# A gated convolution layer on one core: the second root spread goes from four exact products to two rounded ones, and the low halves of the output weights change engines

## The reference, cut to what matters

```
hn = x * rsqrt(mean(x*x) + eps) * norm_g
a, b, gate = split(hn @ w_in)                # 1024 x 3072
u = conv(a * sigmoid(b))                     # depthwise, 31 taps, causal
u = silu(layernorm(u)) * silu(gate)
y = x + u @ w_out                            # 1024 x 1024
```

## Time and profile before

| | |
|---|---|
| median of 3 runs | 363.22 us (363.17 to 363.48) |
| the profiled execution | 363.72 us, its span 361.9 us |
| TensorE busy | 356.9 us, 99% of the span |
| VectorE busy | 319.9 us, 88% |
| GpSimd busy | 269.8 us, 75% |
| ScalarE busy | 232.4 us, 64% |
| granted TensorE clock | 1.00 of full speed |

### The profile page before, as it was taken

How to read it: one execution, slowest core, us unless ns; L and a number is a source line. 1 busy time by engine, 2 the same in 40 slices (tenths; PEclk the granted TensorE clock), 3 DMA queues, 4 the chain that set the end, 5 groups by cost and what they waited for, 6 DMA issues and landing times.

```text
span 361.9 us, 4758 instructions
## 1 busy us (share of the span) xinstructions
PE 356.9 (99%) x1564; PEld 289.2 (80%) x1564; DVE 319.9 (88%) x514; ACT 232.4 (64%) x334; POOL 269.8 (75%) x194
## 2 busy tenths in 40 slices
PE   7999999999999999999999999999999999999996
PEld 6888888888888888888888888888888888888885
DVE  4779799999999899999999998993798979997952
ACT  5889685558847772998667875975655951452400
POOL 0029999999999997899999999795796532359220
PEclk9999999999999999999999999999999999999999
DMA  7995011201411311406112214235713695066042
GB/s 260 403 400 206 34 60 58 91 28 58 116 60 53 65 60 58 116 2 116 58 60 51 67 58 80 96 58 103 246 59 117 237 404 173 0 203 205 31 169 92
DMA packets 30520, 43.51 MB, mean 120 GB/s; under 512 B 18336, under 2 KB 18848, under 8 KB 30496
## 3 DMA queue, kind: packets, MB, share of 16 engines
q1 hardware_dynamic: 30352, 43.21, 37.7%
q10 hardware_dynamic: 144, 0.00, 0.0%
HBM read 34.82 MB, written 4.19 MB: 108 GB/s over the span
## 4 chain that ended last, share of the span: by engine, by line
PE 97%; DMA 1%; SPq 0%; ACT 0%; DVE 0%; issue 0%
PE mm L632 68%; PE acc L711 12%; PE mm L711 9%; PE mm L649 6%; DMA raw<-w_in 1%; PE acc L702 0%; PE acc L692 0%; PE acc L626 0%; ACT w_hi L786 0%; DVE nat L1273 0%; SPq L494 0%; SPq L520 0%; PE acc L620 0%; PE acc L622 0%
## 5 line engine op out<-in xcount | busy, mean ns | idle before, releaser
L632 PE MATMUL mm<-x_hi,w_hi 128*128 128x512 f32 x352 | 139.3, 396 | 0.0
L632 PE MATMUL mm<-x_hi,w_lo 128*128 128x512 f32 x352 | 139.0, 395 | 0.0
L632 PE MATMUL mm<-x_lo,w_hi 128*128 128x512 f32 x352 | 139.0, 395 | 0.0
L1185 DVE SCALAR_TENSOR_TENSOR acc<-u,chan,acc 128x512 f32<-128x512 f32 x157 | 110.7, 750 | 0.1
L632 PEld LDWEIGHTS mm<-x_hi,w_lo 128*128 128x128 f32 x352 | 66.1, 188 | 16.0
L632 PEld LDWEIGHTS mm<-x_hi,w_hi 128*128 128x128 f32 x352 | 66.1, 188 | 15.8
L632 PEld LDWEIGHTS mm<-x_lo,w_hi 128*128 128x128 f32 x352 | 66.1, 188 | 15.8
L1494 POOL TENSOR_TENSOR pconv<-pconv,prod 128x512 f32<-128x512 f32 x60 | 77.3, 1312 | 1.3 <-ACT prod L868 1.3
L1185 DVE SCALAR_TENSOR_TENSOR acc<-u,w_sum,acc 128x512 f32<-128x512 f32 x90 | 67.5, 750 | 1.3 <-ACT acc L850 1.1
L868 ACT ACTIVATE prod<-u,chan 128x512 f32<-128x512 f32 x69 | 47.7, 714 | 15.6 <-POOL pconv L1494 14.3
L1438 POOL TENSOR_TENSOR w_lo<-raw,w_hi 128x1024 fp32r<-128x1024 f32 (+1 forms) x21 | 49.7, 2365 | 9.3 <-ACT w_hi L817 9.2
(11 more groups left out here) (109 smaller groups left out, 541.2 us busy)
## 6 DMA issues: line engine op xcount, KB each, us to landing
raw<-w_in SPq DMA_DIRECT2D x22, 512.0 KB, 3.3
nat<-x_t SPq DMA_DIRECT2D x16, 256.0 KB, 6.1
sgate<-x SPq DMA_DIRECT2D x8, 512.0 KB, 10.8
raw<-w_out SPq DMA_DIRECT2D x8, 512.0 KB, 3.3
nat<-x SPq DMA_DIRECT2D x8, 512.0 KB, 7.9
y<-nat SPq DMA_DIRECT2D x15, 256.0 KB, 2.1
raw_late<-w_out SPq DMA_DIRECT2D x4, 512.0 KB, 4.1
sig<-w_out SPq DMA_DIRECT2D x4, 512.0 KB, 3.9
```

The source lines that it names most:

```text
L632: ins = nc.tensor.matmul(bank(("unit", m, h)), w[:, m % 3, k, :], xx[:, k, half(h)], start=(k == 0 and i == 0), stop=(k == KC - 1 and i == 2))
L1185: ins = nc.vector.scalar_tensor_tensor(dst, chain_in(j, chain, k), tap(j, chain, k), chain_bank(j, chain), ALU.mult, ALU.add)
```

## The change

1. **The roots of half 0.** GpSimd gets `split_rms`: from the roots a rounded copy and the rest (two small instructions, for tiles 0 to 2 and again for tile 3), into `rms_parts`. ScalarE makes two diagonals for each tile instead of one (eight instructions instead of four), in the tile `diags` that half 1 used. TensorE multiplies them in two fp32r products of 512 columns instead of four float32 ones of 128; it waits for all eight ahead of the first.
2. **Low halves of the output weights.** Those of b = 2, 4 and 5 go from GpSimd to VectorE (six instructions of 128x1024). On VectorE b = 2 stands ahead of `add_11`, b = 4 between `sum_v(4)` and `split_v(4)`, b = 5 behind `split_v(5)`, and posts(4, (1,)) moves behind it.
3. **Scales.** `scale(5, 1)` and `scale(7, 1)` go from VectorE to GpSimd, behind a wait for the low parts of b = 0.
4. **Order.** "22-12" waits for eight low parts instead of four; ScalarE does `split_w_out(2, i)` behind the `act_norm` of half 1 instead of ahead of six of them; SyncE issues the reload of the b blocks behind the loads of `spare` and of x's first four row tiles; the reload of the a blocks waits for VectorE's low halves of b = 4.

```diff
-POOL_SCALES = {0: (1, 3, 5, 7), 1: (1, 3)}
+POOL_SCALES = {0: (1, 3, 5, 7), 1: (1, 3, 5, 7)}
...
 W_OPS = [("lo", 0, 0), ("lo", 0, 1), ("lo", 1, 0), ("lo", 1, 1),
-         ("22-12", 2, 0), ("22-12", 2, 1), ("lo", 2, 0), ("lo", 2, 1), ("21-", 3, 0), ("21-", 3, 1),
-         ("lo", 4, 0), ("lo", 4, 1),
-         ("12-11", 5, 0), ("12-11", 5, 1), ("lo", 5, 0), ("lo", 5, 1), ("lo", 6, 0), ("lo", 6, 1)]
+         ("22-12", 2, 0), ("22-12", 2, 1), ("21-", 3, 0), ("21-", 3, 1),
+         ("12-11", 5, 0), ("12-11", 5, 1), ("lo", 6, 0), ("lo", 6, 1)]
...
-W_BY_VECTOR = {("+11", 4, 0): 1, ("+11", 4, 1): 2, ("lo", 3, 0): 3, ("lo", 3, 1): 4}
+W_BY_VECTOR = {("lo", 2, 0): 1, ("lo", 2, 1): 2, ("+11", 4, 0): 3, ("+11", 4, 1): 4, ("lo", 3, 0): 5, ("lo", 3, 1): 6,
+               ("lo", 4, 0): 7, ("lo", 4, 1): 8, ("lo", 5, 0): 9, ("lo", 5, 1): 10}
...
-W_PAUSES = {("22-12", 2, 0): CK, ("lo", 2, 0): 2 * CK, ("21-", 3, 0): 4 * CK, ("12-11", 5, 0): 5 * CK, ("lo", 6, 0): 7 * CK}
+W_PAUSES = {("22-12", 2, 0): 2 * CK, ("21-", 3, 0): 4 * CK, ("12-11", 5, 0): 5 * CK, ("lo", 6, 0): 7 * CK}
...
             def spread_rms(h):
 
+                spread = rms_spread(h).rearrange("p (t q) -> p t q", t=TPH)
+                pe.wait_ge(ones_r_ready, 1)
                 if h == 1:
-                    spread = rms_spread(1).rearrange("p (t q) -> p t q", t=TPH)
-                    pe.wait_ge(ones_r_ready, 1)
                     pe.wait_ge(diag_hi_ready, TPH)
-                    nc.tensor.matmul(spread, ones_r[:], diags[:, 0, :, :], start=True, stop=False)
+                else:
+                    pe.wait_ge(diag_ready, 2 * TPH)
+                nc.tensor.matmul(spread, ones_r[:], diags[:, 0, :, :], start=True, stop=False)
+                if h == 1:
                     pe.wait_ge(diag_lo_ready, TPH)
-                    ins = nc.tensor.matmul(spread, ones_r[:], diags[:, 1, :, :], start=False, stop=True)
-                else:
-                    for i in range(TPH):
-                        pe.wait_ge(diag_ready, i + 1)
-                        ins = nc.tensor.matmul(rms_spread(0)[:, i * P:(i + 1) * P], ones[:], diag(i), start=True, stop=True)
-                ins.then_inc(rms_all_ready, 1)
+                nc.tensor.matmul(spread, ones_r[:], diags[:, 1, :, :], start=False, stop=True).then_inc(rms_all_ready, 1)
...
             def rms_diagonal(t):
 
                 act.wait_ge(ident_in, 16)
-                act.wait_ge(rms_ready, rms_count(t))
-                nc.scalar.activation(diag(t), ident[:], ACT.Copy, scale=rms[:, t:t + 1]).then_inc(diag_ready, 1)
+                act.wait_ge(rms_all_ready, 1)
+                for i in range(2):
+                    act.wait_ge(rms_parts_ready, 2 * (rms_count(t) - TPH - 1) + i + 1)
+                    nc.scalar.activation(diags[:, i, t, :], ident[:], ACT.Copy,
+                                         scale=rms_parts[:, i, t:t + 1].bitcast(F32)).then_inc(diag_ready, 1)
...
+            def split_rms(tiles):
+
+                part = slice(tiles[0], tiles[-1] + 1)
+                done = 2 * (rms_count(tiles[0]) - TPH - 1)
+                pool.wait_ge(rms_ready, rms_count(tiles[0]))
+                nc.gpsimd.tensor_scalar(rms_parts[:, 0, part], rms[:, part], 1.0, 0.0, ALU.mult,
+                                        ALU.add).then_inc(rms_parts_ready, 1)
+                pool.wait_ge(rms_parts_ready, done + 1)
+                nc.gpsimd.tensor_tensor(rms_parts[:, 1, part], rms[:, part], rms_parts[:, 0, part].bitcast(F32),
+                                        ALU.subtract).then_inc(rms_parts_ready, 1)
...
             inverse_rms(range(TPH - 1))
+            split_rms(range(TPH - 1))
             inverse_rms((TPH - 1,))
+            split_rms((TPH - 1,))
...
             for i in range(2):
+                finish_wb_lo(2, i)
+            for i in range(2):
                 add_11(i)
...
             for k in range(CK):
                 sum_v(4, k)
+            for i in range(2):
+                finish_wb_lo(4, i)
             for k in range(CK):
                 split_v(4, k)
             posts(3)
-            posts(4, (0, 1))
+            posts(4, (0,))
             for k in range(CK):
                 split_v(5, k)
+            for i in range(2):
+                finish_wb_lo(5, i)
+            posts(4, (1,))
```

More of the change, by code:

```diff
@@ L152, in gated_conv_layer @@
         half_neg = sb("half_neg", [P, NT])
+        rms_parts = sb("rms_parts", [P, 2, TPH], F32R)
         stats = sb("stats", [P, NT, KC // 2, 6])
@@ L203, in gated_conv_layer @@
         rms_all_ready = sem("rms_all_ready")
+        rms_parts_ready = sem("rms_parts_ready")
         hn_ready = sem("hn_ready")
@@ L458, in half @@
             return slice(h * HALF, (h + 1) * HALF)
-        def diag(i):
-            return sgate[:, i, 0:P]
         def words(columns):
@@ L580, in _ @@
                 load_w_out("a", i, 1, 1)
-            for i in range(2):
-                sp.wait_ge(wb_done, W_OP["22-12", 2, i])
-                load_w_out("b", i, 0, 0)
             sp.wait_ge(unit_ready["g"], NH * KC)
@@ L587, in _ @@
             load_x(0)
+            for i in range(2):
+                sp.wait_ge(wb_done, W_OP["22-12", 2, i])
+                load_w_out("b", i, 0, 0)
             load_x(1)
@@ L592, in _ @@
             for i in range(2):
-                sp.wait_ge(wb_done, W_OP["lo", 4, i])
+                sp.wait_ge(wb_late, W_BY_VECTOR["lo", 4, i])
                 load_w_out("a", i, 0, 0)
@@ L720, in wait_operands @@
                 pe.wait_ge(vlo_ready, CK * b + k + 1)
-                if b == 3:
+                if 2 <= b <= 5:
                     pe.wait_ge(wb_late, W_BY_VECTOR["lo", b, k // 2])
@@ L1050, in _ @@
                 split_v(1, k)
+            for k in range(2, KC):
+                act_norm(k, 1)
             for i in range(2):
                 split_w_out(2, i)
-            for k in range(2, KC):
-                act_norm(k, 1)
             for k in range(CK):
@@ L1210, in add_11 @@
                 dve.wait_ge(wo_in[1][i], 48)
-                dve.wait_ge(wb_done, W_OP["lo", 2, i])
+                dve.wait_ge(wb_late, W_BY_VECTOR["lo", 2, i])
                 nc.vector.tensor_tensor(w_raw("a", i), w_raw("a", i), w_raw("b", i), ALU.add).then_inc(wb_late, 1)
@@ L1535, in _ @@
             for k in POOL_SCALES[1]:
+                if k == CK + 1:
+                    pool.wait_ge(vlo_ready, CK)
                 scale(k, 1)
             for op in W_OPS[4:]:
-                if op == ("lo", 4, 0):
-                    pool.wait_ge(vsum_ready, vsum_count(5, CK - 1))
                 if op in W_PAUSES:
```

## The result

The changed kernel takes 364.28 us (median of 6 runs, 364.11 to 364.44) against 363.20 us for the kernel before (6 runs, 362.49 to 363.48): ratio 1.0029, 95% interval [1.0017, 1.0041]. It is 1.1 us slower; forecast was 0.15 us faster, with a range that ended at 363.75. The profiled execution took 364.37 us with a span of 362.6, against 363.72 and 361.9 before, so the two traces differ by 0.7 us.

What follows compares the result with a forecast made beforehand. TensorE's back-to-back matmuls were taken to bound the kernel from 7.33 us on. Saving 0.43 us and adding 0.28 gave -0.15, from 363.22 to 363.07, said as 363.1 us; range 362.65 to 363.75.

Steps and rivals of the forecast that it cites:

- Part 1, the products: TensorE's spread of half 0: eight float32 records of 0.89 us become two fp32r products of 0.23 us each.
- Gain 0.43, if nothing waits: TensorE's spread of half 0: the cheaper products save 0.89 - 0.46 = 0.43 us if no wait arises.
- the sum: Whole kernel: -0.43 + 0.28 = -0.15 us, taking the median from 363.22 to 363.07 us.
- Part 1, the wait: Ahead of the spread's products TensorE waits for ScalarE's eight diagonals, delayed by GpSimd's held rounding copy: stall 0.24 us.
- 0.13 late: At the spread of half 0, TensorE starts at about 36.90 instead of 36.77 us, 0.13 us late.
- diagonals that end behind 37.2: ScalarE's diagonals for the spread: ending later than 37.2 us would show the prediction wrong; the last was reckoned at 36.85.
- This costs nothing as I see it: Behind the roots: ScalarE's roundings move 1.5 us, GpSimd's low parts about 1.2 us, read from unit 2, half 1; cost 0.
- Parts 2 to 4: Output product's low halves, scales and order: no operand or bank comes late for TensorE, cost 0.
- the tightest place: Output product, VectorE's post of b = 1: done at 307.8 us, bank wanted at 308.30, 0.5 us left.
- slower by VectorE's queue: Rival, output product b = 2: dearer VectorE subtractions delay a post, TensorE stands 0.9 us, 364.0 us; queue case chance 0.13.
- GpSimd slow at the roots: Rival, roots of half 0: subtraction costs what a power costs, stall 0.5 to 0.84, 363.3 to 363.6 us; chance 0.13.

Runs made afterwards that it cites:

- g1: The kernel before with one unused tensor of 32 bytes per partition ahead of the weights' tiles, no instruction changed: 363.78 us, ratio 1.0009 against the kernel before.
- g2: The changed kernel with `rms_parts` allocated last in the first stage, so the weights keep their old addresses: 363.49 us, ratio 0.9993 against the kernel before.
- e1: The changed kernel run again, nothing altered: 364.08 us, ratio 1.0029 against the kernel before.
- f1: The changed kernel with 14 warm-up products instead of 11: 364.47 us, ratio 1.0032 against the kernel before.
- e4: The changed kernel with the spread of half 0 ahead of k = 4 of unit 3 instead of k = 2: 363.52 us, ratio 1.0003 against the kernel before.
- h2: The changed kernel, spread at k = 2 as it is, with the weights shifted by 64 bytes: 361.07 us, ratio 0.9937 against the kernel before.
- h1: The kernel before with 64 unused bytes ahead of the weights' tiles, no instruction changed: 360.18 us, ratio 0.9915 against the kernel before.
- e3: The kernel before with all of the change but the diff of the roots (parts 2 to 4 only): 363.07 us, ratio 0.9994 against the kernel before.
- h4: The changed kernel with the spread at k = 4 and the weights shifted by 128 bytes: 360.53 us, ratio 0.9922 against the kernel before.
- i2: g4 run again, on one chip with i1: 362.49 us, ratio 0.9964 against the kernel before.
- g4: The changed kernel with the spread at k = 4 and 32 unused bytes behind `rms_parts`, a shift of 64: 360.76 us, ratio 0.9935 against the kernel before.
- i1: h1 run again, on one chip with i2: 360.24 us, ratio 0.9917 against the kernel before.
- h3: g2 with VectorE's 128x1024 subtraction one product earlier: 364.33 us, ratio 1.0029 against the kernel before.

## Why the prediction was wrong

- **Part 1, the products.** Right: two records of 0.23 where eight took 0.89.
- **"Gain 0.43, if nothing waits."** This step failed, by a term put at nothing. It took 233 ns as the price of a matmul wherever its operands lie. `rms_parts` moves the weights by 32 bytes; g1, the shift alone, shows 0.33 us for that behind the last spread and 0.0009 of the time (0.3 us), and with the shift no trace has the quicker pace that the middle can have without it (0.89 us where it is met). At the old addresses the whole change is at 0.9993 (g2), about where the sum put it (0.9996). The diff shows the tensor; neither the sum nor a rival mentioned it.
- **Part 1, the wait.** The mechanism was right (the rounding copy held to the end of VectorE's subtraction: 34.65 against 34.60, as reckoned; subtraction 0.19 against 0.22; eight diagonals). The term "0.13 late" was mis-sized: TensorE started 0.71 behind its turn in the first profile, and with the restart (0.08, reckoned 0.11) the stall was 0.79 instead of 0.24. It came 0.10 sooner, the other engines' work there 0.37 later (33.38 against 33.01 for VectorE's subtraction), and it started 0.14 us behind the last diagonal instead of 0.05. The prediction's own sign of being wrong, diagonals that end behind 37.2, came true by 0.04. One profile gave a lateness to the hundredth where its parts move by 0.4 from one execution to the next: the stall was 0.26 in e1, as forecast, and 0.03 and 0.04 in f1 and g2. Over the runs, e4 against e1 prices it at 0.56 us in the medians and 0.9 in the ratios. h2 against h1 prices the change, wait included, at 0.9 us at one address.
- **"This costs nothing as I see it"**, on GpSimd's delay. Followed only to the next reader, unit 2. In the first profile the mean is there at 258.90, before at 257.51, and TensorE takes it at 259.11: 0.2 us of slack where there were 1.3. This pair overstates it: in the other profiles at no shift or one of 32 bytes the slack is 0.3 to 1.5 with part 1 and 0.7 to 1.3 without. At the old pace still free; at a quicker one it is the bound.
- **Parts 2 to 4.** Right: e3 is level with before, no trace has a TensorE wait there, and in the first profile of the changed kernel the tightest place (the post of b = 1, q = 2) was done by 308.2 with its bank wanted at 308.8.
- **The sizes do not quite add up.** Whole against g2 is 0.0036, 1.3 us, on two chips. The last matmuls (0.33) and a quicker middle in some runs (g2 has four of twelve at 362.8 to 362.9, e1 none below 363.8) make some 0.6. With g1 the shift alone comes to 0.3. The rest is inside or just outside the two intervals and stays open.

The rival "slower by VectorE's queue" named the right sign for a wrong reason. "GpSimd slow at the roots" had the first profile's stall in its range (0.5 to 0.84) by luck: its subtraction took 0.19, not what a power takes. The best kernel found is the kernel before with 64 unused bytes: 3.1 us below before.

## What to carry to other kernels

Where TensorE is the whole chain, a new small tile is part of the change: allocate it behind the matmuls' operands, or try the operands at several offsets, before anything else is read from the time. An engine's slack is measured at the present pace: a delay hidden today is the bound as soon as TensorE gets quicker, and a TensorE wait can cost more than its length. Moving an instruction out of one collision is worth trying only after looking at what stands next to it in its new place.

## What the runs showed of the hardware

- The interval between back-to-back 128x128 by 512 fp32r matmuls depends on where the tiles lie in SBUF (with the weights, all that is allocated behind the unused bytes moves): in the projections 233.3 or 232.4 ns (no shift, by execution), 233.3 (32 bytes), 228.9 (64), 226.7 (128); in the output product 233.3, 234.3, 233.3, 226.7. The instructions are the same for h1, g1 and before.
- TensorE's waits of 4.3 us (h4), 3.0 us (i2) and 2.5 us (g4) from start to start were followed by a stretch at a granted clock of one half (1.2 instead of 2.4 GHz), waits of 1.3 to 1.8 us (i1, h1, h2, h3) were not. In i2 the stretch cost 1.6 us beside the wait itself.
- A VectorE instruction with two inputs in SBUF holds a GpSimd instruction that reads SBUF, as the Trainium skill says ("SBUF — State Buffer", section "Who interferes with whom"). This case's traces agree: a rounding copy of three columns took 0.67 us instead of 0.19 (first profile and h3), a power of three columns 1.94 instead of 0.85 (h3 and first profile).
